# A two-block transformer on one core: the order of weight halves behind the experts' last sums and inside the second block's attention

## The reference

```python
def reference(...):
    x = first_block(x, c, w_ada, b_ada, w_in, ...)      # 2 layers
    return second_block(x, mem_2, ...)                  # 2 layers

# first_block, each layer
    mod = cond @ w_ada[l] + b_ada[l]                    # six modulation vectors
    h = _layer_norm(x) * (1.0 + sc1) + sh1
    mix = _mixer(h, ...)
    x = _layer_norm(DN_ALPHA * x + g1 * mix, ln1_g[l], ln1_b[l])
    h = _layer_norm(x) * (1.0 + sc2) + sh2
    ffn = _moe(h, ...)                                  # 16 experts of width 256, 2 of one group per token
    x = _layer_norm(DN_ALPHA * x + g2 * ffn, ln2_g[l], ln2_b[l])

# second_block, each layer
    h = rms_norm(x, norm_mix_g);  proj = h @ w_in
    ret = ...retention of 4 heads...;  pool = ...multiscale pooling...
    na = ...neighbourhood attention, q, k normed, bias table...
    mk, mv = jnp.split(rms_norm(mem, norm_mem_g) @ w_mem_kv, 2, axis=-1)
    mo = memory_attention(mq, mk, mv)
    up = jnp.einsum('bsnc,ncd->bsnd', branches, w_branch)
    merged = jnp.einsum('bsnd,bsnd->bsd', gates, up)    # gates = sigmoid(h @ w_gate)
    x = x + merged @ w_out
    a, g = jnp.split(rms_norm(x, norm_ffn_g) @ w_ffn_in, 2, axis=-1)
    x = x + (jax.nn.silu(a) * g) @ w_ffn_out
```

## Time and profile before

| | |
|---|---|
| median of 3 runs | 1761.6 us (1757.0 to 1761.62) |
| profiled execution, its own time | 1759.37 us |
| its span, first to last instruction | 1757.6 us |
| granted TensorE clock, mean | 0.983 |
| busy: PE, DVE, ACT, POOL | 96%, 66%, 54%, 14% |
| lows on DVE (line 2010) | 310, 711.7 us |
| highs on ACT (line 1398) | 310, 591.1 us |

### The profile page before, as it was taken

The page is one execution under the profiler, slowest core; times in us unless marked ns, Lnnn a source line. Parts: engine busy times, 40 slices in busy tenths (PEclk is TensorE's granted clock), DMA queues, the critical chain, the costliest instruction groups (busy, mean ns, idle before and its releaser), DMA issues.

```text
span 1757.6 us, 25993 instructions
## 1 busy us (share of the span) xinstructions
PE 1692.2 (96%) x10796; PEld 1458.5 (83%) x10796; DVE 1167.7 (66%) x1300; ACT 941.7 (54%) x1067; POOL 238.9 (14%) x209
## 2 busy tenths in 40 slices
PE   6999998999999998999979999999999999999999
PEld 3887886888689896788867889889998889979998
DVE  2647667899965867899986576564547756655453
ACT  4435445877544555688755463453436645445342
POOL 0420020000025002001005402000001710210000
PEclk9999998999999999999999999999999999999999
DMA  9975586999855246799937345456645634536551
GB/s 361 361 258 192 205 315 243 366 366 380 309 165 194 97 140 224 282 375 377 338 112 274 121 126 187 167 176 208 216 168 186 210 121 144 182 130 218 190 192 72
DMA packets 190915, 393.18 MB, mean 224 GB/s; under 512 B 6128, under 2 KB 110576, under 8 KB 174928
## 3 DMA queue, kind: packets, MB, share of 16 engines
q1 hardware_dynamic: 188384, 381.71, 61.9%
q0 software_dynamic: 1712, 7.50, 1.2%
q10 hardware_dynamic: 704, 2.33, 0.4%
HBM read 390.46 MB, written 1.05 MB: 223 GB/s over the span
## 4 chain that ended last, share of the span: by engine, by line
PE 76%; DVE 8%; POOL 6%; ACT 5%; issue 5%; DMA 1%; POOLq 0%; SPq 0%; DVEq 0%; ACTq 0%
PE ps L584 22%; PE ps L586 21%; PE ps L585 21%; DVE low L2010 3%; PE ps L697 2%; ACT whi L1398 2%; POOL TB L2938 1%; PE ps L905 1%; PE ps L873 1%; PE ps L716 1%; PE ps L888 1%; DMA AR<-in_w_ada 1%; PE ps L602 1%; POOL small L2801 1%; DVE Hl L2064 1%
## 5 line engine op out<-in xcount | busy, mean ns | idle before, releaser
L2010 DVE TENSOR_TENSOR low<-raw,whi 128x2048 fp32r<-128x2048 f32 x310 | 711.7, 2304 | 351.5 <-ACT whi L1398 349.4
L1398 ACT ACTIVATE whi<-raw 128x2048 fp32r<-128x2048 f32 x310 | 591.1, 1914 | 326.8 <-PE ps L586 284.1
L584 PE MATMUL ps<-Hh,whi 128*128 128x256 f32 x1536 | 438.7, 286 | 0.0
L586 PE MATMUL ps<-Hh,low 128*128 128x256 f32 x1536 | 434.5, 283 | 0.0
L585 PE MATMUL ps<-Hl,whi 128*128 128x256 f32 x1536 | 434.5, 283 | 0.0
L584 PEld LDWEIGHTS ps<-Hh,whi 128*128 128x128 f32 x1536 | 294.4, 192 | 14.2 <-issue 13.6
L585 PEld LDWEIGHTS ps<-Hl,whi 128*128 128x128 f32 x1536 | 294.5, 192 | 0.6
L586 PEld LDWEIGHTS ps<-Hh,low 128*128 128x128 f32 x1536 | 294.4, 192 | 0.0
L584 PE MATMUL ps<-whi,Hh 128*128 128x512 f32 (+1 forms) x640 | 246.2, 385 | 18.4 <-DVE low L2010 7.5
L586 PE MATMUL ps<-whi,Hl 128*128 128x512 f32 (+1 forms) x640 | 241.5, 377 | 0.0
L585 PE MATMUL ps<-low,Hh 128*128 128x512 f32 (+1 forms) x640 | 241.4, 377 | 0.0
(11 more groups left out here) (341 smaller groups left out, 2168.5 us busy)
## 6 DMA issues: line engine op xcount, KB each, us to landing
raw<-in_w_gu SPq DMA_DIRECT2D x80, 1024.0 KB, 5.3
raw<-in_w_ff SPq DMA_DIRECT2D x66, 1024.0 KB, 5.1
raw<-in_w_in SPq DMA_DIRECT2D x58, 1024.0 KB, 5.4
raw<-in_w_d SPq DMA_DIRECT2D x40, 1024.0 KB, 5.5
raw<-in_w_gate SPq DMA_DIRECT2D x32, 1024.0 KB, 5.4
ada<-in_w_ada SPq DMA_DIRECT2D x16, 1024.0 KB, 6.7
raw<-in_w_out SPq DMA_DIRECT2D x16, 1024.0 KB, 5.1
AR<-in_w_ada SPq DMA_DIRECT2D x13, 1024.0 KB, 8.8
```

The lines of the kernel that those rows point to most:

```text
L584: pe.matmul(out, lhs[0], rhs[0], start=start, stop=False)
L586: return pe.matmul(out, lhs[1], rhs[0], start=False, stop=stop)
L1398: act.activation(wide(i, whi), wide(i, raw), ACT.Copy).then_inc(*up("w_hi", i))
L2010: dve.tensor_tensor(wide(i, low), wide(i, raw), wide(i, whi).bitcast(F32), ALU.subtract).then_inc(*up("w_lo", i))
```

## The change

Two places of the programs of ACT and DVE are reordered. No instruction is added or dropped.

At the end of the experts, in both layers, the loop of tile 19 ends after the halves of d19. Then come the halves of activation 19 (`act_hi`, `act_lo`), the halves of the first following unit, in layer 1 both memory lifts (on ACT behind this half, on DVE one ahead of it and one behind it), the last sum, and only then the halves of the second and third following unit.

In the second block's attention DVE does the first two heads' scores, then the low of `gate (0, 3)`, then the first quotients, then the remainder of retention. Before, the low and the remainder of retention came ahead of the first scores.

```diff
@@ ACT, moe(l): for n in range(NT)
                     taken("A", l, "gu", n, 0)
-                    if n < NT - 1:
-                        silu(n)
+                    if n == NT - 1:
+                        break
+                    silu(n)
                     taken("A", l, "gu", n, 1)
...
                 act_hi(NT - 1)
+                taken("A", l, "gu", NT - 1, 1)
                 if l:
                     mem_lift(0, (0,))
-                taken("A", l, "d", NT - 2)
-                if l:
                     mem_lift(0, (1,))
                 sum_hi(2)
+                taken("A", l, "d", NT - 3)
+                taken("A", l, "d", NT - 2)
@@ DVE, moe(l): for n in range(NT)
                     taken("A", l, "gu", n, 0)
-                    if n < NT - 1:
-                        gated(n)
+                    if n == NT - 1:
+                        break
+                    gated(n)
                     taken("A", l, "gu", n, 1)
-                    if 1 <= n < NT - 1:
+                    if n:
                         act_lo(n - 1)
...
+                act_lo(NT - 1)
                 if l:
                     mem_lift(0, (0,))
-                act_lo(NT - 1)
-                taken("A", l, "d", NT - 2)
+                taken("A", l, "gu", NT - 1, 1)
                 if l:
                     mem_lift(0, (1,))
                 sum_lo(2)
+                taken("A", l, "d", NT - 3)
+                taken("A", l, "d", NT - 2)
@@ DVE, second_block(l)
-                taken("B", l, "gate", 1, 3)
-                dve.wait_ge(*at("ret_hi", l))
-                dve.tensor_tensor(B[1][:, 0:2, :], ps("T", "ret", l)[:, :].rearrange("p (b s) -> p b s", b=2),
-                                  B[0][:, 0:2, :].bitcast(F32), ALU.subtract).then_inc(*up("ret_lo", l))
...
                 scored(0)
+                taken("B", l, "gate", 1, 3)
                 divided(0)
+                dve.wait_ge(*at("ret_hi", l))
+                dve.tensor_tensor(B[1][:, 0:2, :], ps("T", "ret", l)[:, :].rearrange("p (b s) -> p b s", b=2),
+                                  B[0][:, 0:2, :].bitcast(F32), ALU.subtract).then_inc(*up("ret_lo", l))
                 scored(1)
```

## The result

The changed kernel takes 1762.45 us (median of 20 runs, 1761.03 to 1767.8), the kernel before 1760.72 us (20 runs, 1756.73 to 1765.14). The ratio is 1.0014, interval 1.0008 to 1.0020, or 2.5 us more (1.4 to 3.5); the means of the two sets of runs are 2.5 us apart, the medians 1.7. The change costs time, less than half of what I had set as the bound for telling a change from none, and with 20 runs it can be told. The profiled execution has a span of 1759.2 us at a mean clock of 0.982; it is the quickest of the 20.

The account below looks back on a forecast made before the run. PE is busy 96% of the span, so only its waits count, with DVE's queue setting the residual stage. Layer 0 +5.3, layer 1's end +1.8 and attention -3.2 make +3.9 on 1761.6: forecast 1765, range 1760 to 1770.

Parts of the forecast that it names:

- the bound for telling a change from none: Whole kernel: a change under 0.3% (5.3 us) was taken as not to be told from none.
- the base: Whole kernel: median of the three runs shown, 1761.6 us, to which the predicted sum was added.
- Layer 0, +5.3 predicted: End of layer 0's experts: two lows and a wait put half(0, 0) at 475.7, not 470.36; +5.3 us, bounds 4.4 and 5.6.
- PE's waits for modulation weights: End of layer 0's experts: they end before the lift at 482.15, so they don't cover the 5.3 us delay.
- Layer 1's end, +1.8 predicted: End of layer 1's experts: half(0, 0) 0.9 later plus 0.9 for half clock; +1.8 us, from 0.9 to 3.4.
- the half clock at the first lift: Layer 1's end: after 7.5 us of PE idle, eight transposes take 1.94 instead of 1.06; +0.9 us, bounds 0 and 2.5.
- The put-back: Layer 1's end: PE's last put-back can start at about 895.6 instead of about 899.9, 4.3 us early.
- Attention, -3.2 predicted: Second block's attention: PE's waits for two quotients (0.76 and 0.63) go; 1.6 us less a layer, -3.2 for both.
- The bank of the retention's remainder: Rival in attention: the gate waits for this bank, so no attention gain; +7.1, 1768.6; chance 0.2.
- layer 0's delay is absorbed: Rival at layer 0's end: PE's modulation-weight waits give the residual slack, leaving -1.4, 1760; chance 0.08.
- the change does what its name says: Rival at the experts' ends: residual follows the sums, lows cost nothing; -0.2, -4.3 and -3.2, giving 1754; chance 0.04.

Follow-up runs that it names:

- attn_only: The kernel before with the attention edit alone, in both layers; ratio 0.9977 (0.9968 to 0.9986), -4.0 us.
- l1_only: The kernel before with the new order at the end of layer 1's experts alone; ratio 1.0001 (0.9992 to 1.0011), +0.2 us.
- act_first: The kernel before with one DVE swap in layer 1: act_lo(19) between the lows of mkv0 and mkv1; ratio 0.9988 (0.9979 to 0.9996).
- filler_second: The kernel before with 20 thrown-away PE transposes ahead of the second lift of the second block's rows, layer 0; ratio 0.9998 (0.9987 to 1.0009).
- l0_only: The kernel before with the new order at the end of layer 0's experts alone; ratio 1.0032 (1.0020 to 1.0044), +5.6 us.
- l0_three: The changed kernel with a third low, that of vd0, ahead of half(0, 0) on DVE behind layer 0; ratio 1.0031 against the kernel before.
- l0_late: The changed kernel, but behind layer 0 DVE makes the lows of qa1 and ka later than half(0, 0); ratio 0.9998 against the kernel before.
- filled: The kernel before with the attention edit, act_lo(19) earlier in both layers, layer 1's mkv and rqk lows mostly inside lifts; ratio 0.9957, 1753.0 us.
- pe_filler: The changed kernel with 60 thrown-away PE transposes ahead of the first lift of the second block's rows; ratio 1.0023 against the kernel before.

## Why the prediction was right or wrong

I forecast 3.9 us more; it is 2.5 by the times and 2.4 by the traces. In each of the four places the chain was the one that I had laid out, and one term, layer 1's end, was mis-sized. The time that I named, 1765, is 2.6 us above the measured median. Of that 0.9 is the base, 1761.6 from three runs where 20 runs give 1760.72; the rest is the sum.

- **Layer 0, +5.3 predicted.** 5.17 in the trace, 5.6 alone (3.5 to 7.7). The steps are there as laid out: wait for the whi of qa1 (1.11 us), two lows, the first residual row, the lift 5 us later, and PE's wait there released by ACT's rows. One thing I had excluded has a small truth: PE's waits for modulation weights do touch this stage. In executions with the old order the stretch is 26.77, 26.40, 27.65, 28.00 and 27.05 us (before, `attn_only`, `l1_only`, `act_first`, `filler_second`), with a second wait for these weights of 0.42, 0.75, 2.28, 2.62 and 1.64 us; with the new order it is 31.93 to 31.95 in four kernels, with that wait from 0.73 to 2.25. So the new order hides it, and the price is about 4.8 on the mean and not 5.2.
- **Layer 1's end, +1.8 predicted, 0.55 found.** This is the step that was mis-sized, and the 0.55 lies below the bounds that I gave it, 0.9 to 3.4. Two things were too high. `half(0, 0)` comes 0.58 us later and not 0.9, for the greater part since the two sums' high parts took ACT 1.06 us and not the 1.30 of the earlier trace rows. And the half clock at the first lift, which I priced at 0.9, is there (7.45 us of idle, a lift of 1.94 us, granted clock 0.50), but the second lift, at the half level before, is at the full level now and gives it back. I had the row of the lift at 928.92 in the trace and didn't ask which level it had. That it rises is not a chance of one execution: the second lift took 1.94 us in all three kernels with the order before (before, `attn_only`, `l0_only`) and 1.07 in three with the new one (the change, `l1_only`, `l0_three`), with `l0_late` between them at 1.57. But nothing in my working foresaw it, and why it rises is open. The put-back came 4.4 us sooner, as predicted (4.3), and PE's wait was 7.45 (7.5).
- **Attention, -3.2 predicted.** -1.62 and -1.61 in the traces, -4.0 (-5.6 to -2.5) alone. The low lay behind the scores, ACT's table load (1.28 us) and exponentials behind the scores too, as in the working; the remainder of retention ended at 1023.7, and the gate, behind the eight transposes, found its bank free.
- **The rivals.** The bank of the retention's remainder never became a wait. That layer 0's delay is absorbed is excluded by `l0_only` and by `l0_three`. That the change does what its name says is excluded by `half(0, 0)` at 17.12 behind the transposes; `filled` shows what it takes: 3.8 us less in this stage when no low is left between the sum and the residual.

**Where the expected gain of the experts' end went:** 4.4 us on the sums in layer 1, spent on two lows and a wait for their high part; nothing to win in layer 0, where the four lows had lain beside PE's last products, and two of them were moved from this cover into the residual chain.

## What to carry to other kernels

In a queue that keeps its order, work without hurry belongs into waits of the engine, not ahead of the chain that everything waits for; moving it back past one urgent instruction (the last sum) is worth nothing if the next one (the residual) is as urgent. A bracket of 4.47 us on the busiest engine was worth 1.3 us, because the chain ran through another engine's queue. Count from a row that no edit touches, and learn first how well a stretch repeats: layer 1's end and the attention repeated to 0.05 us where whole runs differ by 5 and more, but layer 0's end, in which PE waits for DMA, ran from 26.40 to 28.00 us without an edit.

## What was not expected of the hardware

- PE's level after a short wait isn't told by the wait's length alone. Behind idle stretches of 2.62 us (before, at 928.92) and 2.65 us (after, at 934.68), with the same instructions ahead, the lift ran at the half level in one and at the full level in the other. Behind 2.64 us in `act_first` it was the full level, and behind 2.64 in `l0_late` the lift took 1.57. What decides is left open. The Trainium skill (TensorE: Matmul & The Clock Gate, section What's actually happening) has the level set by how busy the array has been recently. That the last wait alone doesn't decide agrees with it; what in the activity ahead made the difference, none of these rows shows.
- 60 thrown-away transposes (6.71 us) in the place of a wait of 7.45 us kept the lift behind it at the full level (1.04 us in `pe_filler`), and the next lift, 16 us later, fell to the half level as in the kernel before.
